# Expert stage on TensorE: seven prompt sections per expert instead of nine

## The reference, cut to what matters

```
def expert_choice_ffn(x, w_router, w1, w3, w2):
    ...
    cap = EC_FACTOR * n // N_EXPERTS
    aff = jax.nn.softmax((xf @ w_router).astype(jnp.float32), axis=-1)
    top_aff, top_idx = lax.top_k(aff.T, cap)
    xe = xf[top_idx]
    hid = jax.nn.silu(jnp.einsum('ecd,edf->ecf', xe, w1)) * jnp.einsum('ecd,edf->ecf', xe, w3)
    ye = jnp.einsum('ecf,efd->ecd', hid, w2) * top_aff[..., None].astype(xf.dtype)
    out = jnp.zeros_like(xf).at[top_idx.reshape(-1)].add(ye.reshape(-1, d))
```

## Time and profile before

| what | us |
|---|---|
| median of 3 runs (lowest, highest) | 3371.49 (3366.47, 3373.31) |
| the profiled execution, its own time | 3371.65 |
| its span, first to last instruction | 3369.9 |
| PE busy | 3182.6 (94%) |
| DVE busy | 2179.3 (65%) |
| ACT busy | 1657.9 (49%) |

### The profile page before, as it was taken

How to read it: one execution, slowest core, us unless ns; L and a number is a source line. 1 busy time by engine, 2 the same in 40 slices (tenths; PEclk the granted TensorE clock), 3 DMA queues, 4 the chain that set the end, 5 groups by cost and what they waited for, 6 DMA issues and landing times.

```text
span 3369.9 us, 54074 instructions
## 1 busy us (share of the span) xinstructions
PE 3182.6 (94%) x22270; PEld 2439.4 (72%) x22270; DVE 2179.3 (65%) x2735; ACT 1657.9 (49%) x2157; POOL 417.7 (12%) x345
## 2 busy tenths in 40 slices
PE   5997999979899994999999999999999999999998
PEld 2443888878777773777777777777777777777776
DVE  7644233156666547777777777777777777777777
ACT  1103222157411333666666666666666666666665
POOL 2210100033444121000000000000000000000010
PEclk8998999989999996999999999999999999999999
DMA  5464332154676334788777777777778778778786
GB/s 179 168 228 180 111 121 85 69 148 127 251 245 212 136 113 169 278 298 294 271 290 294 274 287 294 273 288 296 271 286 298 270 288 293 271 291 294 272 316 264
DMA packets 226033, 791.13 MB, mean 235 GB/s; under 512 B 28525, under 2 KB 35321, under 8 KB 221564
## 3 DMA queue, kind: packets, MB, share of 16 engines
q1 hardware_dynamic: 206028, 722.02, 58.2%
q0 software_dynamic: 19760, 65.65, 6.6%
HBM read 730.31 MB, written 57.26 MB: 234 GB/s over the span
## 4 chain that ended last, share of the span: by engine, by line
PE 58%; DVE 1%; DMA 1%; ACT 0%; issue 0%; POOL 0%; SPq 0%; ACTq 0%; DVEq 0%
PE exp_bank L2819 15%; PE exp_bank L2821 14%; PE exp_bank L2820 14%; PE exp_bank L2829 14%; PE exp_bank L2801 1%; DMA exp_xb<-residual 1%; PE exp_bank L2803 1%; PE exp_bank L2787 0%; DMA out_y<-exp_xb 0%; DVE exp_lo L2505 0%; DVE g_pick L2372 0%; DVE g_pick L2371 0%; DVE g_pick L2374 0%; DVE exp_xb L2720 0%; ACT exp_hi L2501 0%
## 5 line engine op out<-in xcount | busy, mean ns | idle before, releaser
L2505 DVE TENSOR_TENSOR exp_lo<-exp_raw,exp_hi 128x1024 fp32r<-128x1024 f32 x1056 | 1290.2, 1225 | 272.7 <-ACT exp_hi L2501 179.8
L2501 ACT ACTIVATE exp_hi<-exp_raw 128x1024 fp32r<-128x1024 f32 x1056 | 1119.6, 1062 | 567.0 <-PE exp_bank L2821 557.3
L2819 PE MATMUL exp_bank<-exp_hi,exp_xt 128*128 128x512 f32 (+1 forms) x1536 | 582.6, 379 | 2.2 <-DVE exp_lo L2505 1.3
L2820 PE MATMUL exp_bank<-exp_lo,exp_xt 128*128 128x512 f32 (+1 forms) x1536 | 571.6, 372 | 0.0
L2821 PE MATMUL exp_bank<-exp_hi,exp_xt 128*128 128x512 f32 (+1 forms) x1536 | 571.3, 372 | 0.0
L2819 PEld LDWEIGHTS exp_bank<-exp_hi,exp_xt 128*128 128x128 f32 x1536 | 289.4, 188 | 90.9 <-issue 39.1
L2821 PEld LDWEIGHTS exp_bank<-exp_hi,exp_xt 128*128 128x128 f32 x1536 | 289.6, 189 | 51.2
L2829 PE MATMUL exp_bank<-exp_raw,exp_xtp 128*32 128x256 f32 (+1 forms) x6144 | 324.1, 363 | 0.0
L2820 PEld LDWEIGHTS exp_bank<-exp_lo,exp_xt 128*128 128x128 f32 x1536 | 289.8, 189 | 47.1
L2819 PE MATMUL exp_bank<-exp_hi,exp_hid 128*128 128x512 f32 x704 | 279.9, 398 | 0.7 <-DVE exp_lo L2505 0.7
L2821 PE MATMUL exp_bank<-exp_hi,exp_hid 128*128 128x512 f32 x704 | 274.4, 390 | 0.0
(11 more groups left out here) (415 smaller groups left out, 4302.5 us busy)
## 6 DMA issues: line engine op xcount, KB each, us to landing
exp_raw<-in_w SPq DMA_DIRECT2D x1056, 512.0 KB, 7.3
hy_table<-in_basis_s POOLq DMA_DIRECT2D x64, 512.0 KB, 5.1
carry_tiles<-in_w_ada SPq DMA_DIRECT2D x24, 1024.0 KB, 5.6
proj_raw<-in_w_in SPq DMA_DIRECT2D x24, 512.0 KB, 4.3
filt_table<-in_kbasis_s SPq DMA_DIRECT2D x18, 512.0 KB, 6.3
spectrum_s<-filt_spec SPq DMA_DIRECT2D x34, 256.0 KB, 2.2
carry_flex<-spectrum_s SPq DMA_DIRECT2D x16, 512.0 KB, 3.9
features<-proj_xr SPq DMA_DIRECT2D x12, 512.0 KB, 3.0
```

The source lines that it names most:

```text
L2501: act.activation(st.hi[:, n % st.ns, :], raw(n), ACT.Copy).then_inc(st.hi_done, 1)
L2505: dve.tensor_tensor(st.lo[:, n % st.ns, :], raw(n), st.hi[:, n % st.ns, :].bitcast(F32), ALU.subtract).then_inc(st.lo_done, 1)
L2819: pe.matmul(out, xh, wh, start=(k == 0), stop=False)
L2820: pe.matmul(out, xh, wl, start=False, stop=False)
```

## The change

The list of sections is cut anew, and three tables of chunk numbers with it. Blocks 4 and 5 form one section: PE does the sample products of chunks 32 to 43, then the prompt products of the same twelve. The second layer has two sections, chunks 44 to 54 and 55 to 65. So there are seven sections: four of 8 chunks, one of 12, two of 11. `TURN` moves the transposes of block 3 from chunk 39 to 43, of block 4 from 43 to 49, of block 5 from 51 to 54. `OUT_AT` moves block 4 from chunk 41 to 45 and block 5 from 45 to 51. The rings keep their 16 and 6 slots. No arithmetic is added or removed.

```
-    GROUPS = [(i, c0, c1) for i, (c0, c1, _) in enumerate(UNITS[:NB])] + [(NB, 44, 52), (NB, 52, 59), (NB, 59, NC)]
-    TURN = {15: 0, 23: 1, 31: 2, 39: 3, 43: 4, 51: 5}
+    GROUPS = [[(i, 8 * i, 8 * i + 8)] for i in range(4)] + [[(4, 32, 40), (5, 40, 44)], [(NB, 44, 55)], [(NB, 55, NC)]]
+    TURN = {15: 0, 23: 1, 31: 2, 43: 3, 49: 4, 54: 5}
     TURN_AT = {c + 2: b for c, b in TURN.items()}
-    OUT_AT = {UNITS[b][1] + 1: b for b in range(NB)}
+    OUT_AT = {9: 0, 17: 1, 25: 2, 33: 3, 45: 4, 51: 5}
...
-                for i, c0, c1 in GROUPS:
-                    u = e * NU + i
...
-                    for c in range(c0, c1):
-                        prompts(e, i, c)
+                for group in GROUPS:
+                    for i, c0, c1 in group:
+                        u = e * NU + i
...
+                    for i, c0, c1 in group:
+                        for c in range(c0, c1):
+                            prompts(e, i, c)
```

More of the change, by code:

```diff
@@ L2835, in _ @@
             for e in range(NE):
-                for i, c0, c1 in GROUPS:
-                    u = e * NU + i
[L2838 to L2843, removed]
-                    for c in range(c0, c1):
[L2845 to L2855, removed]
-                        prompts(e, i, c)
+                for group in GROUPS:
+                    for i, c0, c1 in group:
+                        u = e * NU + i
+                        if c0 == UNITS[i][0]:
+                            if u >= 2:
+                                evicted(pe, u - 2)
+                            if i == 0:
+                                pe.wait_ge(s_xlo, e * 2 + 2)
+                                pe.wait_ge(s_xhi, e * 3 + 3)
+                        for c in range(c0, c1):
+                            pe.wait_ge(st.lo_done, e * NC + c + 1)
+                            f = c - UNITS[NB][0]
+                            if i == NB and f % 4 == 0:
+                                pe.wait_ge(s_hid, e * NB + f // 4 + 1)
+                                pe.wait_ge(s_hp, e * NB + f // 4 + 1)
+                            samples(e, i, c)
+                            if c in TURN:
+                                hid_transposes(e, TURN[c])
+                            if c == X_TURN and e < LAST:
+                                x_transposes(e + 1)
+                    for i, c0, c1 in group:
+                        for c in range(c0, c1):
+                            prompts(e, i, c)
             pe.wait_ge(s_lss, 3)
```

## The result

The changed kernel takes 3458.57 us (median of 4 runs, 3457.78 to 3459.41), the kernel before 3369.72 beside it (3366.47 to 3373.31): ratio 1.0265, 95% interval 1.0253 to 1.0277, 89 us more. The forecast was 3452, in a range of 3410 to 3490.

What follows compares the result with a forecast made beforehand. PE was taken to bound the experts. Per expert, wait 3.8 plus low clock 1.7 less section gain 0.45 made 5.05 us; for 16 experts 80.8 on 3371.5, so 3452 us, range 3410 to 3490.

Steps and rivals of the forecast that it cites:

- PE is the bound of the experts: Inside the experts PE is busy 1798.74 of 1800 us and never waits, so each microsecond in its stream counts.
- The wait: Before chunk 44 PE waits for DVE's gated product of block 4: 3.8 us per expert, 3.4 to 4.9.
- the landing of chunk 49: Chunk 49's load lands 4.1 to 5.6 us after issue; 4.5 taken, so 5.65 us after the prompt products start.
- The clock: Behind each wait the granted clock falls to about 0.5 for about 3.5 us, costing 1.7 us per expert.
- the case of 698 us: Earlier idle stretch, 698 to 702 us, followed by clock 0.50 for 5.2 us; by it the fall costs 2.6 us.
- the first case: Earlier idle stretch, 1253 to 1257 us, followed by clock 0.52 for 3.5 us; by it the fall costs 1.7 us.
- The gain of two sections: Two fewer prompt sections per expert save 0.72 us, less 0.27 for transposes: net 0.45 us, between 0.34 and 0.72.
- two packs of transposes: Block 4's and the next tokens' transposes, now between sample products, cost 0.27 us per expert, between nothing and 0.38.
- The gain of 0.72: Upper end of the sections' gain per expert, if the 128-wide transposes cost nothing extra, as by the Trainium skill.
- The clock holds: Rival, chance 0.20: clock does not fall behind the waits; 3.35 us per expert, 3425 us in all.
- Faster: Rival, chance 0.05: PE does not wait at chunk 44, leaving only the 7 us gain; 3364 us.
- A second wait: Rival, chance 0.13: late loads or late ACT and DVE stop PE again at chunks 54 to 60; 3476 us.

Runs made afterwards that it cites:

- out43: The changed kernel with block 4's silu and gated product at chunk 43 of the ACT and DVE streams instead of 45; 3366.42 us, ratio 0.9987.
- out44: The changed kernel with block 4's silu and gated product at chunk 44 instead of 45; 3395.07 us, ratio 1.0074.
- filled: The changed kernel with seven extra matmuls, result never read, in PE's stream where it waits before chunk 44; 3422.89 us, ratio 1.0166.
- twelve_only: The changed kernel with the second layer in three sections again, keeping the section of twelve chunks; 3445.32 us, ratio 1.0231.

## Why the prediction was right, point by point

- **PE is the bound of the experts, so each wait is in the time.** It held: the distance between two experts grew from 126.6 to between 130.8 and 133.4 us, 5.4 in the mean of experts 2 to 15, which is the wait of 3.7, the low clock behind it, and the sections saved.
- **The wait.** Predicted 3.8 us per expert (3.4 to 4.9) from the landing of chunk 49 through one split, three operations of DVE and PE's start; measured 3.7 (3.2 to 4.8, eight of the sixteen below 3.4). The releaser, its place and the row of ACT that waits for the landing are those of the prediction. out43 and out44 show the cause and not just the coincidence.
- **The clock.** Predicted 1.7 us per expert, from a low stretch of 3.5 us; measured 2.2 (filled, 35.7 / 16; 1.9 by the traces). This is the term that was too small. In nine of sixteen cases 5.4 to 6.1 us of matmuls ran at the low level, close to the case of 698 us in the earlier trace rows, which I had kept as the upper end. That waits of this length are nearest the first case was not borne out: waits of 3.2 to 3.5 us had either kind behind them.
- **The gain of two sections.** Predicted 0.45 us per expert, between 0.34 and 0.72; measured 0.63. I had priced two packs of transposes between sample products at 0.27 us. They cost nothing extra. A pack of six after the change, and the sample products behind it:

```profile
2089.60 0.60 PE L2801 MATMUL exp_bank<-g_ident,exp_hd 128*128 128x128 f32 x4
2090.03 0.38 PE L2803 MATMUL exp_bank<-g_ident,exp_hdp 128*128 128x128 f32 x2
2090.17 0.47 PE L2819 MATMUL exp_bank<-exp_hi,exp_hid 128*128 128x512 f32 x1
2090.49 0.39 PE L2820 MATMUL exp_bank<-exp_lo,exp_hid 128*128 128x512 f32 x1
```

  The pack takes 0.57 us and the product behind it 0.32 instead of 0.23, together 0.66 over the product itself; at a section's end a pack takes 2068.49 - 2067.75 = 0.74. The drain of the Trainium skill ("TensorEngine Tiling (Array Packing)", Key Properties) at a change of tiling mode was the better guide to what the packs cost. The gain of 0.72, worked out from rows with nothing for them, is nearer to the 0.63 than mine.
- **The sum.** 3.7 + 2.2 - 0.63 = 5.27 us, times 16 = 84, of the 89 measured. Of the other 5 some 2 are the last expert, which beyond its own wait and clock loses more in each kernel whose last expert has the section of twelve; the rest isn't told from the spread of the runs. I had weighed it at nothing; in out43, where nothing else is left, it is 8 us. Part of the nearness to 3452 is luck: the clock was priced 0.5 us too low per expert and the gain 0.18 too low, which pull against each other; and the landing of chunk 49 was put between two values, where the mean of ten waits of 3.2 to 3.5 us and six of 3.7 to 4.8 happens to lie.
- **The rivals.** The clock holds: wrong here, half right in twelve_only. Faster: it needed the product by 5.3 us after the prompt products' start; it came at 8.5 to 10.1. (The shortest time from issue to landing of a chunk in the trace before is 3.1 us, not the 4.1 named there, which is short only among second loads; 3.1 would have been too late as well.) A second wait in the eleven-chunk sections: none, but for the last expert.

## What to carry to other kernels

When work is moved later in an engine's stream, ask what it now stands behind: here the product of a block moved past the splits of two chunks whose loads the same change had held back, and one number in a table was worth 92 us. A ring's depth limits a section not only by capacity: the section, the work ahead, and whatever the next unit waits for must all lie inside it. And when PE waits, count the clock too: a wait of 3.7 us cost 5.6 to 5.9.

## What was not expected of the hardware

- Added matmuls made the kernel 36 us faster (31 by the traces), since they kept the granted clock at 1.00 through a wait.
- Of eleven waits of 3.2 to 3.5 us in twelve_only eight left the clock at 1.00; in the changed kernel all waits of this length lowered it; a wait of 2.6 us in out43 lowered it too, as did one of 1.9 us in out44, whose fifteen others of 1.3 to 2.6 us did not.
- How long the clock stayed low wasn't set by the length of the wait: of the sixteen waits of the changed kernel nine had 5.4 to 6.1 us of matmuls at the low level behind them, seven 3.3 to 3.4, and both kinds stood behind waits of 3.2 to 3.5 us.
